# A block on one core: TensorE multiplies one block of the modulation weights, and the first projection uses its low weights last

## The reference

```python
mod = jax.nn.silu(c) @ w_ada + b_ada                    # c: 1024, w_ada: 1024 x 6144
shift_m, scale_m, gate_m, shift_f, scale_f, gate_f = jnp.split(mod, 6, axis=-1)
h = rmsnorm(x, g_mix_pre) * (1.0 + scale_m[:, None]) + shift_m[:, None]
z = h @ w_in                                            # q, k, v, forget logits, pool, conv, gates
```

## Time and profile before

| | |
|---|---|
| median of three runs | 788.3 us |
| the profiled execution, whole | 788.2 us |
| its span, first to last instruction | 787.0 us |
| TensorE busy | 773.3 us, 98% |
| VectorE busy | 568.7 us, 72% |
| ScalarE busy | 437.8 us, 56% |
| GpSimd busy | 75.4 us, 10% |
| granted clock of TensorE | 1.00 in the first stage's stretches |

### The profile page before, as it was taken

How to read it: one execution, slowest core, us unless ns; L and a number is a source line. 1 busy time by engine, 2 the same in 40 slices (tenths; PEclk the granted TensorE clock), 3 DMA queues, 4 the chain that set the end, 5 groups by cost and what they waited for, 6 DMA issues and landing times.

```text
span 787.0 us, 11513 instructions
## 1 busy us (share of the span) xinstructions
PE 773.3 (98%) x4504; PEld 672.3 (85%) x4504; DVE 568.7 (72%) x776; ACT 437.8 (56%) x652; POOL 75.4 (10%) x128
## 2 busy tenths in 40 slices
PE   6999999999999999999999999999999999999997
PEld 5999877888898888888899997889988988888885
DVE  4986999859787567676667998657647666665664
ACT  5555487675665444444465477656646644444452
POOL 5023930000010000000020001100001100000001
PEclk9999999999999999999999999999999999999999
DMA  9989998945457686765566654446433765666651
GB/s 322 367 271 295 361 316 297 337 164 162 133 168 238 199 299 191 268 216 183 169 185 212 172 161 150 160 142 211 157 92 103 221 200 188 188 189 194 190 175 54
DMA packets 84533, 163.35 MB, mean 208 GB/s; under 512 B 5424, under 2 KB 15856, under 8 KB 84480
## 3 DMA queue, kind: packets, MB, share of 16 engines
q1 hardware_dynamic: 82656, 157.31, 61.4%
q10 hardware_dynamic: 1424, 4.81, 1.8%
q0 software_dynamic: 400, 0.50, 0.3%
HBM read 161.55 MB, written 1.05 MB: 207 GB/s over the span
## 4 chain that ended last, share of the span: by engine, by line
PE 94%; DVE 2%; ACT 2%; issue 1%; DMA 1%; SPq 0%; POOL 0%; DVEq 0%; ACTq 0%; POOLq 0%
PE bank L1859 20%; PE bank L1861 20%; PE bank L1860 20%; PE bank L1929 13%; PE bank L1932 7%; PE bank L1872 2%; PE bank L1879 2%; PE bank L1874 2%; DVE ada_acc L1046 1%; PE bank L1982 1%; PE bank L2560 1%; PE bank L2133 1%; DMA ada_ring<-in_w_ada 1%; PE bank L2156 1%; PE bank L2020 0%
## 5 line engine op out<-in xcount | busy, mean ns | idle before, releaser
L1016 DVE TENSOR_TENSOR lo_ring<-raw_ring,hi_ring 128x1024 fp32r<-128x1024 f32 x247 | 303.0, 1231 | 150.6 <-ACT hi_ring L540 149.9
L540 ACT CAST hi_ring<-raw_ring 128x1024 fp32r<-128x1024 f32 x248 | 260.0, 1051 | 250.4 <-PE bank L1861 145.9
L1859 PE MATMUL bank<-hi_ring,branch_hi 128*128 128x512 f32 x352 | 139.0, 395 | 0.0
L1860 PE MATMUL bank<-lo_ring,branch_hi 128*128 128x512 f32 x352 | 137.2, 390 | 0.0
L1861 PE MATMUL bank<-hi_ring,branch_lo 128*128 128x512 f32 x352 | 137.0, 389 | 0.0
L1929 PE MATMUL bank<-h_hi_lo,hi_ring 128*128 128x512 f32 x448 | 111.8, 392 | 0.0
L1929 PEld LDWEIGHTS bank<-h_hi_lo,hi_ring 128*128 128x128 f32 x448 | 81.3, 189 | 15.1
L1861 PEld LDWEIGHTS bank<-hi_ring,branch_lo 128*128 128x128 f32 x352 | 66.1, 188 | 14.0
L1859 PEld LDWEIGHTS bank<-hi_ring,branch_hi 128*128 128x128 f32 x352 | 66.1, 188 | 13.9 <-issue 0.8
L1860 PEld LDWEIGHTS bank<-lo_ring,branch_hi 128*128 128x128 f32 x352 | 66.2, 188 | 13.4 <-issue 0.5
L1859 PE MATMUL bank<-h_hi_lo,hi_ring 128*128 128x256 f32 x240 | 69.2, 288 | 0.0
(11 more groups left out here) (300 smaller groups left out, 1161.1 us busy)
## 6 DMA issues: line engine op xcount, KB each, us to landing
raw_ring<-in_w_ff SPq DMA_DIRECT2D x128, 512.0 KB, 3.7
raw_ring<-in_w_in SPq DMA_DIRECT2D x64, 512.0 KB, 4.8
raw_ring<-in_w_out SPq DMA_DIRECT2D x16, 512.0 KB, 3.3
raw_ring<-in_w_xkv SPq DMA_DIRECT2D x16, 512.0 KB, 3.6
mem_v<-in_w_ada SPq DMA_DIRECT2D x13, 512.0 KB, 5.0
mem_k<-in_w_ada SPq DMA_DIRECT2D x11, 512.0 KB, 5.3
ada_ring<-in_w_ada SPq DMA_DIRECT2D x8, 512.0 KB, 7.2
raw_ring<-in_w_branch SPq DMA_DIRECT2D x8, 512.0 KB, 3.4
```

Of the source, the lines that this page charges most:

```text
L540: act.copy(m.hi[:, m.slot(u)], m.raw[:, m.slot(u)]).then_inc(s.hi_done, 1)
L1016: dve.tensor_tensor(m.lo[:, m.slot(u)], m.raw[:, m.slot(u)], as_f32(m.hi[:, m.slot(u)]), ALU.subtract).then_inc(s.lo_done, 1)
L1859: pe.matmul(out, a_hi, b_hi, start=start, stop=False, skip_group_check=True)
L1860: pe.matmul(out, a_hi, b_lo, start=False, stop=False, skip_group_check=True)
```

## The change

Five edits, all in the first stage.

- **One product on TensorE.** Load 3 of w_ada has the last two blocks of quarter 0. VectorE skips the second of them (seven products instead of eight). TensorE multiplies it by itself, raw block as stationary operand and silu column as moving one: four matmuls that open the sums, before VectorE's accumulator is added to them. The load that overwrites this slot waits for it too.
- **Columns chunk by chunk.** Quarter 0's sums go to two banks (6 for chunk 0, 0 for chunk 1), with a semaphore each; VectorE makes gain and shift of one chunk at a time. Run-up: two matmuls instead of six after the transposes, one instead of three ahead of the first unit. Unit 0's v slab writes to bank 7 instead of 4.
- **Rounded chunk first.** ScalarE makes the rounded chunk straight from its source in one instruction, and then the float32 one in another from the same source. VectorE's low part waits for both.
- **Low weights last.** A lead does all products with the rounded h and hi weights, then lo weights, per chunk, and those with the low part of h at the end. The other slabs do the sixteen products with hi weights first and the eight with lo weights then. They begin once the hi half is there, and wait for the lo half in the middle. The column sums of the next quarter stand behind the first of the eight.
- **VectorE's and ScalarE's order.** Four of a quarter's products stand between the second and the third low half, two between the first and the second, two beside the chunk lows. The chunks of the next quarter are made on ScalarE ahead of the cast of unit 4q + 5, instead of behind it.

```diff
+ADA_DIRECT = 3, 1
...
-        self.xm, self.mem = Turn(turns, True), Turn(turns, True)
+        self.xm, self.mem = Turn(turns, True, made=KD), Turn(turns, True)
...
             sp.wait_ge(s.ada_used, ada_before(a) + 1)
+            if ada_before(a) == ADA_DIRECT[0]:
+                sp.wait_ge(s.mix_cols_ps, 1)
...
+    def affine(turn, k, src):
+        for dst, done in ((m.h_hi, turn.hi), (m.h_f32, turn.made)):
+            act.activation(dst[:, k, :], src, ACT.Identity, bias=m.adacol[:, k:k + 1],
+                           scale=m.adacol[:, 8 + k:9 + k]).then_inc(done.sem, 1)
...
-    affine_quarter(0)
+    act.wait_ge(*s.xm.turned.at(1))
+    for k in range(UK):
+        act.wait_ge(s.mix_cols if k else s.first_cols, 2)
+        affine(s.xm, k, m.chunk_ps(k))
...
         hi(u + 4)
+        affine_quarter(q + 1)
         hi(u + 5)
-        affine_quarter(q + 1)
...
-        ada_ops[0] += 1
+        ada_ops[0] += 1 if i != UK * ADA_DIRECT[0] else UK
...
+    def first_columns(chunk, b, done_ps, done):
+        def both_rows(buf, at):
+            return buf[:, at:at + 16].rearrange("p (a b) -> p a b", b=8)[:, :, chunk]
+        dve.wait_ge(done_ps, 1)
+        dve.tensor_tensor(both_rows(m.adacol, 0), bank[b][:, 0:2], both_rows(cols, B_ADA), ALU.add).then_inc(done, 1)
+        dve.wait_ge(done, 1)
+        scale = m.adacol[:, 8 + chunk:9 + chunk]
+        dve.scalar_tensor_tensor(out=scale, in0=scale, scalar=1.0, in1=cols[:, G_MIX + chunk:G_MIX + chunk + 1],
+                                 op0=ALU.add, op1=ALU.mult).then_inc(done, 1)
...
-    for _ in range(KD):
+    for _ in range(KD - 1):
         ada()
+    first_columns(0, 6, s.first_cols_ps, s.first_cols)
     dve.wait_ge(s.hi_done, 1)
...
-    norm_columns(0, 0)
+    first_columns(1, 0, s.mix_cols_ps, s.mix_cols)
...
-        for _ in range(2 * UK if q else UK):
+        for _ in range(UK):
             ada()
         lo(u + 2)
-        for _ in range(UK):
+        for _ in range(2 * UK):
             ada()
         lo(u + 3)
-        for _ in range(UK):
-            ada()
+        norm_columns(q + 1, 4)
 
         lo(u + 4)
-        norm_columns(q + 1, 4)
-
+        for k in (UK * q + 2, UK * q + 3):
+            shifted_lo(s.xm, k)
+            if q < RING - 2:
+                ada()
         lo(u + 5)
-        affine_lo(s.xm, (q + 1,))
...
+    def split_features(u, j, x_hi, x_lo, b0, beside=None):
...
+        for k, kc, fc, out, start in tiles:
+            pe.matmul(out, m.hi[:, slot, k, fc], x_hi[:, kc, :], start=start, stop=False, skip_group_check=True)
+            pe.matmul(out, m.hi[:, slot, k, fc], x_lo[:, kc, :], start=False, stop=False, skip_group_check=True)
+        pe.wait_ge(s.lo_done, u + 1)
+        for i, (k, kc, fc, out, _) in enumerate(tiles):
+            mm = pe.matmul(out, m.lo[:, slot, k, fc], x_hi[:, kc, :], start=False, stop=j == RING - 1 and k == UK - 1,
+                           skip_group_check=True)
+            if beside:
+                beside(i)
+        mm.then_inc(s.used, 1)
...
-    run_up(6)
+    run_up(2)
...
-            if i == (4 if q == 1 else 0):
+            if i == 0:
                 norm_columns(q, 4)
...
-    norm_columns(0, 0)
-    run_up(3)
+    claim(0, 6)
+    a, k = ADA_DIRECT
+    pe.wait_ge(s.silu_ok, 1)
+    pe.wait_ge(s.ada_in[a], 2 * DMA)
+    for b, chunk in ((6, 0), (0, 1)):
+        first_sums(b, chunk, m.ada_raw[a][:, k, :], m.silu_c[:, UK * a + k:UK * a + k + 1], True, False)
+    pe.wait_ge(s.ada_used, RING)
+    for b, chunk, done in ((6, 0, s.first_cols_ps), (0, 1, s.mix_cols_ps)):
+        first_sums(b, chunk, m.ada_acc[:, 0, :], m.ones[:, 0:1], False, True).then_inc(done, 1)
+    free[0], free[6] = (s.mix_cols, 1), (s.first_cols, 1)
+    run_up(1)
```

More of the change, by code:

```diff
@@ L271, in __init__ @@
             new("pad_zero"))
-        self.lo_first = new("lo_first")
+        self.lo_first, self.first_cols_ps, self.first_cols = new("lo_first"), new("first_cols_ps"), new("first_cols")
         self.ones_ok = new("ones_ok")
@@ L651, in affine_quarter @@
         act.wait_ge(s.mix_cols, 2 * q + 2)
-        if q:
-            act.wait_ge(s.x_turned, q)
-        affine_hi(s.xm, m.adacol[:, 8:16], m.adacol[:, 0:8], (q,), (lambda k: m.h_f32[:, k, :]) if q else m.chunk_ps)
-    affine_quarter(0)
+        act.wait_ge(s.x_turned, q)
+        for k in (UK * q, UK * q + 1):
+            affine(s.xm, k, m.h_f32[:, k, :])
+    act.wait_ge(*s.xm.turned.at(1))
+    for k in range(UK):
+        act.wait_ge(s.mix_cols if k else s.first_cols, 2)
+        affine(s.xm, k, m.chunk_ps(k))
     for q in range(RING - 1):
@@ L1047, in ada @@
                                            op1=ALU.add)
-        if k == 0 and n == 1:
+        if k == 0 and n == 1 and a != ADA_DIRECT[0]:
             own.mark(ins)
@@ L1091, in made_lo @@
                           ALU.subtract).then_inc(turn.lo.sem, 1)
[L1093 to L1096, removed]
     def take_half(u_end, b, dst, sem):
@@ L1881, in lead_features, with lead_tokens @@
         return mm
-    def lead_tokens(u, k0, x_hi, x_lo, outs, first, last, turn, claims=()):
-        pe.wait_ge(s.lo_done if u else s.lo_first, u + 1)
+    def lead_tokens(u, k0, x_hi, x_lo, outs, first, last, turn, claims):
+        pe.wait_ge(s.hi_done, u + 1)
         slot = m.slot(u)
         for k in range(UK):
-            if k and not u:
-                pe.wait_ge(s.lo_done, 1)
             pe.wait_ge(*turn.hi.at(k0 + k + 1))
             for tt in reversed(range(NT)):
-                if k == 0 and claims:
+                if k == 0:
                     claim(claims[tt])
@@ L1896, in lead_tokens @@
                           skip_group_check=True)
+            pe.wait_ge(*((s.lo_first, 1) if u == k == 0 else (s.lo_done, u + 1)))
+            for tt in reversed(range(NT)):
+                tok = slice(tt * P, tt * P + P)
                 pe.matmul(outs[tt], x_hi[:, k0 + k, tok], m.lo[:, slot, k, :], start=False, stop=False,
                           skip_group_check=True)
+        for k in range(UK):
             pe.wait_ge(*turn.lo.at(k0 + k + 1))
@@ L1904, in lead_tokens @@
         return mm
+    def split_features(u, j, x_hi, x_lo, b0, beside=None):
+        pe.wait_ge(s.hi_done, u + 1)
+        slot = m.slot(u)
+        tiles = [(k, UK * j + k, slice(f * P, f * P + P), bank[b0 + f // 2][:, (f % 2) * S:(f % 2) * S + S],
+                  j == k == f % 2 == 0) for k in range(UK) for f in range(4)]
+        for k, kc, fc, out, start in tiles:
[8 more added lines that the diff above has]
+        mm.then_inc(s.used, 1)
     def unit_features(u, k0, x_hi, x_lo, banks, first, last, tiles=4, beside=None):
@@ L2056, in pe_program @@
     turn_normed(s.xm)
-    run_up(6)
+    run_up(2)
     for b in range(4):
-        free[4 + b] = s.xm.hi.at(2)
+        free[4 + b] = s.xm.made.at(2)
         if b:
@@ L2102, in cumulative, with first_sums @@
         free[6], free[7] = (s.cum_out, 1), (s.key_sums, 1)
-    norm_columns(0, 0)
-    run_up(3)
+    def first_sums(b, chunk, w, rhs, first, last):
+        for i in range(2):
+            c = (2 * i + chunk) * P
+            mm = pe.matmul(bank[b][:, i:i + 1], w[:, c:c + P], rhs, start=first and i == 0, stop=last,
+                           skip_group_check=True)
+        return mm
+    claim(0, 6)
[9 more added lines that the diff above has]
+    run_up(1)
     for q in range(RING):
@@ L2112, in pe_program @@
             if i == 2:
-                lead_tokens(u, UK * q, m.h_hi, m.h_lo, (bank[4][:, :], bank[5][:, :]), (True, q == 0),
-                            (True, q == RING - 1), s.xm, (4, 5)).then_inc(s.used, 1)
-                free[4] = (s.v_part, q + 1) if q < RING - 1 else (s.v_sum, q)
+                b = 4 if q else 7
+                lead_tokens(u, UK * q, m.h_hi, m.h_lo, (bank[b][:, :], bank[5][:, :]), (True, q == 0),
+                            (True, q == RING - 1), s.xm, (b, 5)).then_inc(s.used, 1)
+                free[b] = (s.v_part, q + 1) if q < RING - 1 else (s.v_sum, q)
             else:
@@ L2120, in pe_program @@
                     beside = next_columns(q + 1) if q < RING - 1 else forget_logits
-                features(u, q, m.h_hi, m.h_lo, 2 * i, beside=beside)
+                split_features(u, q, m.h_hi, m.h_lo, 2 * i, beside)
             if u == 13:
```

17 lines of the change are left out of this document (4 added, 13 removed).

## The result

The changed kernel takes 790.46 us (median of 20 runs, 787.68 to 791.90), the kernel before 788.26 (20 runs, 787.85 to 788.88): ratio 1.0027, with a 95% interval of 1.0021 to 1.0033. It is slower by 0.27%. The forecast was 787.3, with a range up to 789.0, and slower had a chance of 0.05.

The account below looks back on a forecast made before the run. TensorE, busy 98% of 787.0 us, was taken as the bound. Start -2.2, old holes -0.68 and -0.49, unit 3's low weights +0.6, leads +1.6 and +0.2, VectorE +0.1 sum to -0.9: 787.3 us, range 785.7 to 789.0.

Parts of the forecast that it names:

- A rule that speaks against it: At the start, run-up matmuls cut from thirteen to seven: no cost charged, despite a warning that idle gaps halve TensorE's clock.
- third rival: TensorE's clock falls back at the start, losing 1.9 to 3.0 us, so 789.2 to 790.3; chance 0.07.
- units 1 to 3, low weights last: In these units, the same 24 matmuls, 0.12 apart, take 2.88 us a unit, so the reordering adds no term.
- the forecast's sum: All terms over the first stage: start, old holes, unit 3's low weights, leads and VectorE, together -0.9 us, giving 787.3.
- Start: TensorE's first product starts at 15.9 against 17.67, and unit 1 at 18.7 against 20.92: 2.2 us gained.
- the bound of 0.3: At the start, TensorE's product of the eighth w_ada block costs 0 to 0.3 depending on its landing; 0 taken.
- Unit 1's load: Before unit 1's cast, the load was taken to land at 17.1; worst case 18.38, costing 0.75.
- Unit 3's low weights: In unit 3, low weights wanted at 26.4 are ready at 26.9: a new wait of 0.5 to 0.6, 0.08 for restart.
- Leads: At units 4, 8 and 12, 0.45 of waiting and 0.08 of restart each, 1.6 together; second chunks 0.2 together.
- Rival 1: The start's gain survives whole: leads don't wait and unit 3's low is in time; 785.2 to 785.6, chance 0.12.
- Unit 13 "about 1 us earlier": A sign that the forecast is right: the thirteenth unit starts about 1 us earlier.
- rival 2: VectorE sets the pace, 0.8 in each of two rounds, 788.9; or unit 1 lands late, 788.0; together chance 0.19.

Follow-up runs that it names:

- e1: The changed kernel with the old run-up counts (six after the transposes, three ahead of the first product); 789.51 us, ratio 1.0018.
- e3: The changed kernel with the edits of e1 and e2 together: old run-up counts and unit 15 in the old form; 788.70 us, ratio 1.0007.
- e8: The changed kernel with all slabs in the old form, low weights inside every unit, the rest kept; 789.47 us, ratio 1.0015.
- e4: The kernel before with only the run-up cut (six to two, and three to one); 790.32 us, ratio 1.0020.
- e2: The changed kernel with unit 15 in the old form, low weights inside, so forget-logit matmuls stand apart as before; 788.75 us, ratio 1.0008.
- e5: e2 with the next quarter's column sums issued earlier, after 12 of the unit's 16 high-weight matmuls; 786.03 us, ratio 0.9973.
- e7: The kernel before with only unit 15 regrouped: low weights last, forget-logit matmuls between them; 790.39 us, ratio 1.0026.
- e6: e5 with run-up matmuls where TensorE waits: three after the transposes, one before the sums, two ahead of the first product; 785.39 us, ratio 0.9963.

## Why the prediction was wrong

The failed step is the one headed **A rule that speaks against it**: the run-up cut from thirteen to seven matmuls was costed at nothing and the third rival given 0.07, because an idle 0.6 had not dropped the clock before. In before that idle time had twelve run-up records ahead of it and six behind it; the change took both sides of that cover away and put sixteen one-column records in. The row was read for the length of the gap alone, without what stood around it. With the full run-up the fall at the start is in no trace (e1, e3); with the cut one it stands in after, e8 and e4, though not in e2 and e5, and e2 has five low clocks in eleven runs where e3 has one in twelve. In after it costs 1.5 us, where the sum had nothing.

The rule cited there (the Trainium skill, TensorE: Matmul & The Clock Gate, "Why this matters for your kernels") speaks of idle gaps longer than the 0.37 of after, so by its own words it foresaw neither fall; the prediction cites it without that condition. Here the length of the gap alone does not sort the kernels: before idled 0.61 ahead of its sums and held, after idled 0.37 and fell, and ahead of the second fall no idle time is shown at all. The measurement decides.

A second step failed without being weighed at all: the part on units 1 to 3, low weights last, says "The same 24 matmuls, 0.12 apart, 2.88 us a unit, so no term by itself", and I let that stand for unit 15 too, whose logits lie beside its low products. The count of matmuls is the same, but not the company they keep. e7 and e2 show it from both sides. With the first fall alone the forecast's sum would be 787.3 + 1.4 = 788.7, inside its range; it took both falls to bring the time to 790.46.

With sizes from the profiled runs, after against e2: the first fall costs 1.52 from the first product to unit 1 (20.67 - 16.26 = 4.41 against 18.73 - 15.84 = 2.89). The first product was 0.42 late besides, before the clock fell, and 0.58 was absorbed, most of it at unit 3's low weights, for which after no longer waits. That leaves 59.17 - 57.81 = 1.36 at unit 13. The second fall costs (2.65 - 1.44) = 1.21 in the first twelve matmuls of the next unit, and some 0.35 in the last group of logits, 1.56. So -1.13 (58.94 to 57.81) + 1.36 + 1.56 = 1.79 at the row where the trace shows 1.80. The median lies 2.2 above before, not 1.8, since the runs at 0.992 have more of the low level than the profiled one with 0.995; where, no trace shows.

The rest of the working held, by e2's trace and the two undisturbed runs of after. Their spans, 785.9 and 786.0, are 1.0 to 1.1 below the 787.0 of before, where the forecast's sum is 0.9. Their times are only 0.5 below the median of before, since 1.8 us of each lies outside the span, and 1.2 in the profiled run of before.

- Start: 15.9 forecast, 15.84 measured; unit 1 at 18.7 and 18.73. In after TensorE did wait 0.27 for the w_ada block, inside the bound of 0.3, and then 0.37 more for VectorE. Unit 1's load: its cast starts at 17.06 in e2 with no idle time before it, so the load had landed by then, as the 17.1 that I took.
- Unit 3's low weights: 26.9 forecast, 26.88 measured; the wait, 0.33 + 0.16, is 0.49 against 0.5 to 0.6.
- Leads: 0.45 forecast; 0.24 idle by the same way of counting is 0.40. The extra wait for the second chunk does not appear. Rival 1 is out: leads do wait, until the sums are moved (e5). Its own sum was also 0.2 too high; its terms give 785.0 to 785.4.
- Unit 13 "about 1 us earlier": 1.13. VectorE as the pacer (rival 2): the low weights of units 7 and 11 are not waited for in e2, and leads there are 12.87 apart (29.23, 42.09, 54.97), as the 12.8 worked out.

So the third rival came true in its mechanism and place, with a price of 1.5 instead of 1.9 to 3.0: the fall lasted 3.4 us, not 3.8 to 6.1. That its 789.2 to 790.3 lies close to the measured 790.46 is luck, since the second fall was in none of its terms.

What stays open: which of the thin pieces (the one-column records, the short idle stretches, the eight-column groups) a fall needs, since the runs changed them together; why it comes in some runs and not in others; and the runs at 0.991 and 0.993 in e2 and e3 (794.41 and 793.19), which lost more than any traced one. On the second there is a hint: of the traces of the change's cut start, the two that fell have idle time ahead of both groups of one-column matmuls (after 0.27 and 0.37, e8 0.30 and 0.35), the two that held, e2 and e5, have none there. These are four traces, and whether the idle time is the cause is not shown. Of e2's spread of 1.3 us at a clock of 0.999 and 1.000, 0.8 is in the spans (786.3 to 787.1) and the rest outside them. The Trainium skill (the same page, "What's actually happening") says of the slow stretch at a kernel's start that it varies from run to run for one and the same kernel. That is the warm-up and not a later fall; for the falls, the runs of after show the same, with two of 20 undisturbed.

## What to carry to other kernels

Matmuls that only keep TensorE running have a price in both directions: count them as part of the start, and put them where the engine waits anyway (e6); more of them than fit there hold up the first product (e3). When products are regrouped, look at which small matmuls come to stand together, and read the granted clock of each stretch and of every run before any wait, since a busy share of 100% hides a halved clock. The clock column has a limit too: it reads 1.00 over the first burst of the earlier trace rows, whose matmuls run at half the pace of the later ones. A sum whose result takes 2 us to come round belongs that far ahead of its use: moving it up by five matmuls took 2.3 us off (787.68 to 785.35, the profiled runs of e2 and e5).

## What the hardware did that I had not expected

The clock fell while TensorE was shown busy without a break, by ends that are modelled: in e7 its busy time is 5.00 of 5.00 in 66 to 71 us, in groups of four 128x8 and one 128x256 matmul per 0.57 us, and at 71.6 the clock goes to 0.50; before, with three 128x256 matmuls per 0.80 us between the same groups, it stayed at 1.00. And a fall of 3.4 us costs 1.5 to 1.6 us where it happens, in a 788 us kernel, 0.2%, so that it looks like scatter until the runs are sorted by clock.
